# A two-stack transformer kernel: the second stack's attention rewritten over pairs of heads, with half of the index search inside it

## The reference, cut to what matters

```python
def second_block(x, ...):                      # for l in range(2):
    h = rms_norm(x, attn_norm_g[l]); proj = h @ w_in[l]
    (mq, mk, mv, dq, dk, dv, sq, sk, sv, iq, ik, iw) = split(proj)
    # q and k of all three parts: per-head rms norm, then rope
    moba = moba_attention(...)                 # 4 heads of 64; causal here
    # differential: 4 heads, two q/k sets, values 128 wide, causal
    a = softmax(q1 k1 / 8) - lam * softmax(q2 k2 / 8)
    diff = rms_norm(a @ v, subln) * (1 - lam_init)
    # DSA: 4 heads; a query sees only the top 128 causal keys by an index score
    score = sum_h iw[h] * relu(iq[h] . ik / 8); score = where(causal, score, -inf)
    _, sel = top_k(score, 128)
    dsa = softmax(q k / 8 over sel) v
    x = x + concat(moba, diff, dsa) @ w_out[l]
    h2 = rms_norm(x, ffn_norm_g[l])
    x = x + (silu(h2 @ w_gate[l]) * (h2 @ w_up[l])) @ w_down[l]
```

## Time and profile before

| | |
|---|---|
| time, three runs | 2916.03, 2920.96, 2920.37 us (median 2920.37) |
| the profiled execution's own time | 2935.62 us |
| its span in the trace | 2932.9 us |
| TensorE busy | 2559.4 us (87%), weight loads 2096.6 us (71%) |
| VectorE busy | 1541.6 us (53%) |
| ScalarE busy | 1225.5 us (42%) |
| GpSimd busy | 676.3 us (23%) |

### The profile page before, as it was taken

How to read it: one execution, slowest core, us unless ns; L and a number is a source line. 1 busy time by engine, 2 the same in 40 slices (tenths; PEclk the granted TensorE clock), 3 DMA queues, 4 the chain that set the end, 5 groups by cost and what they waited for, 6 DMA issues and landing times. The chain is left out here.

```text
span 2932.9 us, 34627 instructions
## 1 busy us (share of the span) xinstructions
PE 2559.4 (87%) x12840; PEld 2096.6 (71%) x12840; DVE 1541.6 (53%) x2890; ACT 1225.5 (42%) x2448; POOL 676.3 (23%) x364
## 2 busy tenths in 40 slices
PE   6989886975989796965997989999979978899998
PEld 6877765755877675755685667888866856688886
DVE  1844657844745647844498842332225987333322
ACT  2435625753436626742553632222135446222221
POOL 3400314763400314752351110000023502000000
PEclk9988887997989987985999989999979999999999
DMA  4110017953210017952220013222211200222221
GB/s 142 55 47 1 1 52 270 352 215 138 69 47 1 1 59 295 358 216 86 72 87 15 1 65 105 101 86 94 83 58 58 98 4 18 77 100 87 101 79 65
DMA packets 53797, 283.02 MB, mean 96 GB/s; under 512 B 13056, under 2 KB 13056, under 8 KB 27008
## 3 DMA queue, kind: packets, MB, share of 16 engines
q1 hardware_dynamic: 44416, 264.03, 25.0%
q0 software_dynamic: 9216, 16.80, 1.5%
HBM read 274.49 MB, written 23.07 MB: 101 GB/s over the span
## 5 line engine op out<-in xcount | busy, mean ns | idle before, releaser
L185 ACT ACTIVATE weights_hi<-weights_raw 128x2048 fp32r<-128x2048 f32 (+5 forms) x138 | 240.9, 1746 | 683.3 <-PE ps L208 619.1
L195 POOL TENSOR_TENSOR weights_lo<-weights_raw,weights_hi 128x2048 fp32r<-128x2048 f32 (+5 forms) x60 | 261.5, 4358 | 807.8 <-ACT weights_hi L185 807.2
L195 DVE TENSOR_TENSOR weights_lo<-weights_raw,weights_hi 128x2048 fp32r<-128x2048 f32 (+3 forms) x78 | 165.5, 2122 | 533.9 <-ACT weights_hi L185 533.9
L206 PE MATMUL ps<-y2t_hi,weights_hi 128*128 128x512 f32 x704 | 283.0, 402 | 10.2 <-PEq L1622 10.2
L208 PE MATMUL ps<-y2t_hi,weights_lo 128*128 128x512 f32 x704 | 278.8, 396 | 0.0
L207 PE MATMUL ps<-y2t_lo,weights_hi 128*128 128x512 f32 x704 | 277.5, 394 | 0.0
L206 PE MATMUL ps<-weights_hi,attn_ht_hi 128*128 128x512 f32 (+2 forms) x576 | 218.3, 379 | 9.4 <-PEq L229 5.5
L207 PE MATMUL ps<-weights_lo,attn_ht_hi 128*128 128x512 f32 (+2 forms) x576 | 214.8, 373 | 0.0
L208 PE MATMUL ps<-weights_hi,attn_ht_lo 128*128 128x512 f32 (+2 forms) x576 | 214.7, 373 | 0.0
L206 PEld LDWEIGHTS ps<-y2t_hi,weights_hi 128*128 128x128 f32 x704 | 133.2, 189 | 41.4 <-DVE weights_lo L195 10.9
L208 PEld LDWEIGHTS ps<-y2t_hi,weights_lo 128*128 128x128 f32 x704 | 133.1, 189 | 34.6
(11 more groups left out here) (450 smaller groups left out, 6017.6 us busy)
## 6 DMA issues: line engine op xcount, KB each, us to landing
weights_raw<-in_stream SPq DMA_DIRECT2D x108, 1024.0 KB, 4.8
weights_raw<-in_expert_gu SPq DMA_DIRECT2D x34, 1024.0 KB
expert_raw<-in_expert_gu SPq DMA_DIRECT2D x30, 1024.0 KB
expert_raw<-in_expert_down SPq DMA_DIRECT2D x18, 1024.0 KB, 8.1
weights_raw<-in_expert_down SPq DMA_DIRECT2D x14, 1024.0 KB
weights_raw<-in_stream SPq DMA_DIRECT2D x12, 960.0 KB, 4.7
ln_more<-expert_rows SPq DMA_DIRECT2D x16, 512.0 KB, 7.7
weights_raw<-in_stream SPq DMA_DIRECT2D x8, 700.0 KB, 12.5
```

Of the source, the lines that this page charges most:

```text
L185: self.nc.scalar.activation(self.split_tiles(u)[0][:, 0:n], self.env.raw[:, u % self.RAW, 0:n], ACT.Copy).then_inc(self.hi_ready, 1)
L195: eng.tensor_tensor(lo[:, 0:n], self.env.raw[:, u % self.RAW, 0:n], hi[:, 0:n].bitcast(F32), ALU.subtract).then_inc(self.lo_ready, 1)
L206: nc.tensor.matmul(out, a[0], b[0], start=start, stop=False, **more)
```

## The change

`attention_stage` loses its masks, its two-units-together order and its side work; only the first block still calls it, with the same operations as before. The second block gets `pair_attention_stage`, which goes over 32 pairs of heads (two heads of one query tile: 16 differential, 8 MoBA, 8 DSA).

- Masks are added by TensorE: an identity times the mask (both in float32r, which needs one record) is accumulated onto the scores; 128 columns for the causal mask, all nk columns for the index mask of the DSA pairs with t >= 1.
- One reduction over both PSUM banks of a pair gives both negated maxima. The scale 1/8 is now in q, put there by the copies to `qk_t`.
- For a differential pair the two probability tiles are merged before the transposition: p1 + p2 * (lambda * sum1 / sum2). One transposition, one copy and one value product then serve both heads. GpSimd's lambda work is gone.
- Eight of the 16 search rounds go into the attention loop: in each of the first 24 iterations VectorE does MAX8 and MATCH_REPLACE8 for one tile, with a wait behind each; in iteration 24 the three masks are written, and TensorE's DSA scores wait for them.
- The other eight rounds stand behind the first three rotations of the projection stage (2, 3 and 3), none behind the last.
- The squares, the root and the scaling of the differential part go from the last iterations to iterations 20 to 25 of 32.

In iteration i TensorE does the scores of pair i (into two of four banks, after the exponentials of pair i - 2), the transpositions of pair i - 2 (one bank if it was merged, else two) and the value products of pair i - 3; VectorE does the maximum of pair i, the merge of pair i - 1, the search step and the result of pair i - 4; ScalarE does the copies of pair i - 2 and the exponentials of pair i.

The core of the diff:

```diff
+class IndexSearch:
+    TAKEN, ROUNDS, LATE = -3e38, N_TOP // 8, 8
...
+    def take(self, link, t):
+        v, score = self.env.nc.vector, index_score(self.proj, t)
+        link(v.max(self.top[:, t, :], score))
+        link(v.match_replace(score, self.top[:, t, :], score, self.TAKEN))
+    def step(self, dve, link, i):
+        if i < self.LATE * len(self.tiles):
+            self.take(link, self.tiles[i % len(self.tiles)])
+        if i == self.LATE * len(self.tiles):
+            for t in self.tiles:
+                self.env.nc.vector.tensor_scalar(self.mask(t)[0], index_score(self.proj, t), self.TAKEN, MASKED,
+                                                 ALU.not_equal, ALU.mult).then_inc(self.masked, 1)
...
-                ROUNDS = N_TOP // 8
-                share = ROUNDS // len(normed)
+                ROUNDS = N_TOP // 8 - late_rounds
                 for i in range(len(normed)):
                     rotate_job(i)
                     if i + 1 < len(normed):
                         invert(i + 1)
-                    find_top(range(i * share, (i + 1) * share if i + 1 < len(normed) else ROUNDS))
-                for t in tiles:
-                    v.tensor_scalar(index_score(proj, t), index_score(proj, t), TAKEN, MASKED, ALU.not_equal, ALU.mult)
+                        find_top(range(i * ROUNDS // (len(normed) - 1), (i + 1) * ROUNDS // (len(normed) - 1)))
...
+def pair_attention_stage(env, stage, pairs, lam, search, diff_end, prefetch):
+            def _(pe):
+                for i in range(N + 3):
+                    if i < N:
+                        if i >= 2:
+                            pe.wait_ge(exp_done, 2 * (i - 1))
+                        if wide:
+                            pe.wait_ge(search.masked, u["mask"][1])
+                        for h in range(2):
+                            nc.tensor.matmul(score(i, h), u["q"][h], u["k"][h], start=True, stop=False)
+                        for h in range(2):
+                            out = score(i, h) if wide else score(i, h)[:, nk - P:nk]
+                            last = nc.tensor.matmul(out, env.ident_r, u["mask"][0] if wide else env.causal_r, start=False,
+                                                    stop=True)
+                        last.then_inc(scores_ready, 1)
...
+            def _(dve):
+                for i in range(N + 4):
+                    if i < N:
+                        dve.wait_ge(scores_ready, i + 1)
+                        v.tensor_reduce(top[:, i, :], ps[:, 2 * (i % 2):2 * (i % 2) + 2, 0:nk], AX, ALU.max, negate=True
+                                        ).then_inc(max_ready, 1)
+                    if 1 <= i < N + 1 and pairs[i - 1]["merge"]:
+                        dve.wait_ge(exp_done, 2 * j + 2)
+                        link(v.reciprocal(recip[:, j, :], total[:, j, :]))
+                        link(v.scalar_tensor_tensor(out=ratio[:, j:j + 1], in0=recip[:, j, 1:2], scalar=total[:, j, 0:1],
+                                                    in1=lam, op0=ALU.mult, op1=ALU.mult))
+                        v.scalar_tensor_tensor(out=prob[:, j % 3, 0, 0:nk], in0=prob[:, j % 3, 1, 0:nk],
+                                               scalar=ratio[:, j:j + 1], in1=prob[:, j % 3, 0, 0:nk], op0=ALU.mult, op1=ALU.add
+                                               ).then_inc(merged, 1)
+                    search.step(dve, link, i)
...
+            def _(act):
+                for i in range(N + 2):
...
+                    if i < N:
+                        act.wait_ge(max_ready, i + 1)
+                        for h in range(2):
+                            nc.scalar.activation(prob[:, i % 3, h, 0:nk], score(i, h), ACT.Exp, bias=top[:, i, h:h + 1],
+                                                 accum_out=total[:, i, h:h + 1]).then_inc(exp_done, 1)
+                    diff_end.scalar(act, i, out_stored)
...
-                transpose_stage(env, "qk_t", [([proj[:, t, c:c + P] for t in range(T)], qk_t[:, n, :], None)
-                                              for n, c in enumerate(cols)])
+                transpose_stage(env, "qk_t", [([proj[:, t, c:c + P] for t in range(T)], qk_t[:, n, :],
+                                               HD ** -0.5 if is_q[n] else None) for n, c in enumerate(cols)])
```

More of the change, by code:

```diff
@@ L361, in _, with attention_stage @@
                     store(ends.index(n - 2))
-def attention_stage(env, stage, units, scale, prob=None, prob_t=None, prefetch=0, meanwhile=None, together=1):
-    nc, ps, ident, causal = env.nc, env.ps, env.ident, env.causal
+def attention_stage(env, stage, units, scale, prob, prob_t, prefetch):
+    nc, ps, ident = env.nc, env.ps, env.ident
     N = len(units)
@@ L395, in _ @@
                 for i in range(N + 4):
-                    if i < N and i % together == 0:
-                        if i + together > 4:
-                            pe.wait_ge(exp_done, i + together - 4)
-                        for j in range(i, i + together):
-                            nc.tensor.matmul(score_bank(j, units[j]["nk"]), units[j]["q"], units[j]["k"], start=True,
-                                             stop=True).then_inc(scores_ready, 1)
+                    if i < N:
+                        u = units[i]
+                        if i >= 4:
+                            pe.wait_ge(exp_done, i - 3)
+                        nc.tensor.matmul(score_bank(i, u["nk"]), u["q"], u["k"], start=True, stop=True
+                                         ).then_inc(scores_ready, 1)
                     if 3 <= i < N + 3:
@@ L2433, in pool, with __init__ @@
-    def pool(self, pool, out_stored):
-        g = self.env.nc.gpsimd
-        pool.wait_ge(out_stored, self.after)
-        for t in range(T):
-            g.tensor_scalar(self.d2[:, t, :], self.d2[:, t, :], self.lam, None, ALU.mult).then_inc(self.combined, 1)
-        for t in range(T):
-            pool.wait_ge(self.combined, t + 1)
-            g.tensor_tensor(self.d1[:, t, :], self.d1[:, t, :], self.d2[:, t, :], ALU.add).then_inc(self.combined, 1)
+    NH, W, FIRST = 4, 128, 20
+    def __init__(self, env, ctx, y):
+        self.env, self.y = env, y
+        tile = lambda name, *shape: ctx.enter_context(env.nc.sbuf_tensor(name, [P, *shape], F32, allow_name_mangling=True))
+        self.squares, self.ss = tile("diff_squares", self.NH, self.W), tile("diff_ss", T, self.NH)
+        names = ("squared", "root", "inverse")
+        self.squared, self.root, self.inverse = (env.sem("diff_end", n) for n in names)
@@ new lines, in second_layer, with half @@
+                search = IndexSearch(env, heads, proj)
+                def half(chunk, side, a, b):
+                    return qk_t[side * HD:(side + 1) * HD, chunk, a:b]
+                pairs = []
+                for name, n_pairs, q0, k0, v0, y0, w in (("diff", 4, 4, 8, B_DV, B_DQ, 2 * HD),
+                                                         ("moba", 2, 0, 2, B_MV, B_MQ, HD), ("dsa", 2, 12, 14, B_SV, B_SQ, HD)):
+                    for n in range(n_pairs):
+                        for t in range(T):
+                            nk = (t + 1) * P
+                            merge = name == "diff"
+                            vs = [v0 + n * P + h * w for h in range(1 if merge else 2)]
+                            pairs.append(dict(
+                                merge=merge, nk=nk, q=[half(q0 + n, h, t * P, nk) for h in range(2)],
+                                k=[half(k0 + n, h, 0, nk) for h in range(2)],
+                                v=[[proj[:, b, c:c + w] for b in range(t + 1)] for c in vs],
+                                dst=proj[:, t, y0 + n * P:y0 + (n + 1) * P],
+                                mask=search.mask(t) if name == "dsa" and t in search.tiles else None))
@@ L2528, in second_layer @@
+                diff_end = DiffEnd(env, heads, proj[:, :, B_DQ:B_DQ + 512])
+                pair_attention_stage(env, "attn2", pairs, lam[:, 0:1], search, diff_end, first_out + 3)
             yt = pair_tile(nc, local, "y2t", KD, S, side="right")
```

175 lines of the change are left out of this document (116 added, 59 removed).

## The result

The changed kernel takes 2881.9 us (median of four; 2879.1 to 2883.2) against 2918.2 for the kernel before: 36.3 us less. The measured ratio is 0.9862, 95% interval 0.9841 to 0.9883; the quotient of the two medians is 0.9876, inside it. The forecast was 2890 in a range of 2878 to 2910, from a gain of 31.

A forecast was written before the change was run, and what follows sets the result against it. Attention had VectorE and TensorE both nearly full; at its border with projection the core waited some 14 us a layer for VectorE's search. 27.9 + 3.2 + 0.5 - 0.6 = 31 took 2920.4 to 2889.4, said as 2890, range 2878 to 2910.

The forecast's parts named there:

- The gap: Between projection and attention: TensorE's first transposes start 15.0 and 12.9 us earlier in the two layers, gain 27.9 us.
- The cover of 11 us: End of the projection stage: VectorE would end near 1552, some 11 us before ScalarE.
- The stage now ends with ScalarE: End of the projection stage: ScalarE's last copy releases the transposes at 1563.7 instead of 1578.7, 15.0 us earlier.
- The transposes: First transposes after the projection stage: full clock after the shorter gap saves 1.6 us a layer, 3.2 in all.
- Those of the result: Transposes of the attention result (y2_t): gain of 0.5 us at most from a warmer end.
- The attention stage: Second block's attention: 103.6 us a layer against 103.3, no change (+0.6 in all), bounds 99 and 111.
- Rival 1: Differential part: lower clock costs 4 to 12 us a layer; time 2898 to 2914, say 2905; chance 0.22.
- the squares: ScalarE's squares and root tables, moved into the attention loop: 2.5 us late per layer.
- Rivals 2, 3 and 4: 2: low clock throughout, 2957 (0.05); 3: tighter loop or VectorE-ended projection, 2905 to 2920 (0.06); 4: ScalarE bound, 2904 (0.06).
- rival 5: Attention loop faster through better overlap, search fitting into waits: 99 us a layer, time 2881; chance 0.10.
- The Trainium skill's price of a table switch: Attention stage: about 2.66 us a switch with the drain; extra switches cost up to 5 us more in two layers.

The follow-up runs named there:

- e3: Changed kernel with its eight early search rounds placed four and four behind the first two rotations instead of two, three and three; median 2886.1 us.
- e11: Changed kernel with the sixth weight split of each second-block projection stage done in four instructions of 128x512; median 2875.2 us.
- e12: Changed kernel without the end of the differential part (squares, root with two table loads, reciprocal, four GpSimd scalings); median 2876.9 us.
- e5: Changed kernel with four search rounds in the loop instead of eight, as twelve takes in iterations 12 to 23, twelve rounds in projection; median 2872.1 us.

## Where the prediction was right, and which step failed

- **The gap** (27.9): right to the tenth in both layers, and so was its reason, with ScalarE's last copy releasing the next stage.
- **The cover of 11 us** between VectorE's and ScalarE's end: 2.7 in truth. VectorE ends 196.0 us after the first projection product (I had 192.3): with another spacing of its rounds, two more of its rotation steps fell beside weight splits, 5.01 and 5.14 us in place of 0.69. ScalarE ends 198.6 us after it (I had 203.7). So the cover was mis-sized by 8 us, and that the term held with 2.7 us to spare was luck.
- **The step that failed: "The stage now ends with ScalarE: the transposes can start at 1563.42 + 0.30".** It took ScalarE's and TensorE's end over from before. But they waited for VectorE there as well, through GpSimd: inversion, scaling, split. So the projection stages gained 36.2 us where I had 27.9. Two, three and three rounds in place of four took that wait away, 5.8 us with the clock behind it, shown by e3, in which it is back. The other 2.7 are scatter of the clock at a wait that both kernels have. The weight stalls of 1.7 and 2.2 us were in the trace of before, and I put them at nothing without a reason.
- **The transposes** (-3.2): -3.0. They follow a gap of 0.94 us and have a clock of 1.00. Those of the result had -0.5, and came to -0.5.
- **The attention stage** (103.6, bounds 99 to 111): 105.3 and 105.5, +4.2 in place of +0.6. This is the second term that was mis-sized, and it hid nearly half of the first. The prices held: maxima 418, 690, 958 and 1220 ns, merges 352 to 752, a take 1.14 of 1.2. The differential part took 51.1 us from its first maximum to MoBA's first, for 50.4: the first group 10.2, the others 13.1, 14.2 and 13.6 for my 12.6, since VectorE still waits for scores 3.8 us; in the first layer of e11, at the higher clock, the last three took 12.6, 13.0 and 12.7. MoBA and DSA with the 0.9 us ahead of the first maximum took 54.3 for 53.2, and out of wrong parts: nothing for the squares (e12) where I had 2.5, and more for the pairs.
- **Rival 1** (lower clock in the differential part, 0.22): the mechanism came, with 0.76 there, and its price was lower. VectorE is 89% busy in this half, so most of TensorE's slower work lies beside it. It cost between 2.5 and 4 us a layer by e11, not 4 to 12, and its time of 2898 to 2914 didn't come.
- **Rivals 2, 3 and 4** did not come. Of rival 5 only the size came, from another place. The Trainium skill's price of a table switch (ScalarE: Activation LUTs, Table sets) with its 5 us for the two layers: e12, with the squares and the root left out, shows nothing to be gained, so here they lie beside other work.
- **What the sum hid.** I booked 27.9 us for the search's move and +0.6 for the loop, where the rewrite's gain and the search's price had cancelled: 103.3 to 84.6 by the one, back to 105.4 by the other. By the forecast's own prices (4.8 us of takes in each of four groups, 38.4 us in two layers, against 27.9 + 3.2) the move was a loss of 7 us; the runs say 4 by the rest and 7 by medians of two batches. The numbers were there, and I didn't set them against each other.

## What to carry to other kernels

Work moved from behind the bound of one stage into another stage is priced by what the second stage's bound engine has free, pair by pair: a take cost 1.15 us beside VectorE-bound pairs and 0.63 where eight of twelve stood beside TensorE-bound ones. It took 1.05 us of search out of the projection stage, and that stage got only 9.6 us shorter for twelve of them in e5, 0.8 each. Move only as much as closes the gap and fits, and price the two halves of a combined change apart, since one may be paying for the other. An engine's end is not its own as long as it waits through a third engine's queue for the one whose work is taken away: follow each wait of the bound engine, however short, to what stands behind it, and add what the clock can take after it. Before you explain a few us by the change, look whether a kernel with the same instructions in that stage has them too.

## What the runs showed of the hardware

- A VectorE operation with two SBUF inputs of 0.69 us takes 5.14 beside a GpSimd instruction of 4.62, and 1.73 to 1.78 beside pieces of a quarter of that; two small copies take 4.77 and 2.59. A MATCH_REPLACE8 beside a split keeps its time. One instruction cut in four made the two projection stages 3.6 and 5.1 us shorter.
- A wait of 1.75 us on TensorE in the middle of dense products was followed by windows of 4 us at a granted clock of 0.69 and 0.88 in one layer of e3; behind the same wait of 1.74 in the other layer the clock stayed at 1.00. Waits of 0.94 between two stages left it at 1.00.
- The same 194 TensorE records of the differential part beside the same work of VectorE (46 us) took 51.1 us at a mean clock of 0.76, 50.0 at 0.81 and 48.6 at 0.88. Filler products lifted the stage's clock from 0.85 to 0.98 and 0.97 and changed its time by +0.5 and -0.8 us; as they load TensorE themselves, that doesn't price the clock.
